# An mLSTM recurrence in chunks: chunk-end maxima found first, each chunk's weights one chunk ahead, loads in two sets

## What is computed

```python
def step(carry, inp):
    C, n, m = carry
    qb, kb, vb, ib, fb = inp
    b = jnp.cumsum(fb, axis=-1)
    d = jnp.where(causal, b[..., :, None] - b[..., None, :] + ib[..., None, :], -jnp.inf)
    inter = b + m[..., None]
    m_t = jnp.maximum(jnp.max(d, axis=-1), inter)
    dexp = jnp.exp(d - m_t[..., None])
    iexp = jnp.exp(inter - m_t)
    s = jnp.einsum('bhtd,bhsd->bhts', qb, kb) * dexp
    num = jnp.einsum('bhts,bhse->bhte', s, vb) + iexp[..., None] * jnp.einsum('bhtd,bhde->bhte', qb, C)
    den = jnp.sum(s, axis=-1) + iexp * jnp.einsum('bhtd,bhd->bht', qb, n)
    h = num / jnp.maximum(jnp.abs(den), jnp.exp(-m_t))[..., None]
    b_last = b[..., -1]
    w_s = b_last[..., None] - b + ib
    m_new = jnp.maximum(b_last + m, jnp.max(w_s, axis=-1))
    wexp = jnp.exp(w_s - m_new[..., None])
    cexp = jnp.exp(b_last + m - m_new)
    C_new = cexp[..., None, None] * C + jnp.einsum('bhs,bhsd,bhse->bhde', wexp, kb, vb)
    n_new = cexp[..., None] * n + jnp.einsum('bhs,bhsd->bhd', wexp, kb)
    return (C_new, n_new, m_new), h
```

## Time and profile before

| | |
|---|---|
| runs of the kernel | 6958.89, 6976.05 and 6981.98 us, median 6976.05 |
| profiled execution, its time | 6989.38 us |
| its span | 6987.6 us |
| mean granted clock of PE | 0.881 of full speed |
| PE busy | 5603.2 us (80%) |
| DVE busy | 2333.7 us (33%) |
| ACT busy | 1178.4 us (17%) |
| DMA moved | 813.87 MB |

### The profile page before, as it was taken

One profiled execution on the slowest core, in us unless ns is written; L12 is line 12 of the kernel. 1 busy time (PEld: TensorE's weight loads), 2 busy tenths in 40 slices (PEclk: granted clock), 3 DMA queues, 4 the chain that ended last, 5 costly groups with the idle time before them and its releaser, 6 DMA issues. The chain is left out here.

```text
span 6987.6 us, 96082 instructions
## 1 busy us (share of the span) xinstructions
PE 5603.2 (80%) x39658; PEld 3068.0 (44%) x39658; DVE 2333.7 (33%) x3925; ACT 1178.4 (17%) x1918; POOL 301.6 (4%) x320
## 2 busy tenths in 40 slices
PE   7998858894986548688859989889558998867778
PEld 4554443332456425233334338888524444322233
DVE  2334310003205643100045365555442120443331
ACT  1222100001110020000023122222201110422111
POOL 0000000001010000000010000000000000211100
PEclk9998869996998757799969999999879999889989
DMA  2110155553133330654332243232231222467721
GB/s 103 36 36 31 60 200 203 220 199 129 48 110 102 111 120 26 244 218 184 146 100 84 80 135 67 53 70 53 73 114 39 57 71 82 145 228 260 254 103 63
DMA packets 559787, 813.87 MB, mean 116 GB/s; under 512 B 176648, under 2 KB 308104, under 8 KB 558920
## 3 DMA queue, kind: packets, MB, share of 16 engines
q1 hardware_dynamic: 491272, 629.25, 27.0%
q0 software_dynamic: 28544, 103.82, 4.2%
q10 hardware_dynamic: 39616, 75.51, 3.0%
HBM read 967.67 MB, written 209.26 MB: 168 GB/s over the span
## 5 line engine op out<-in xcount | busy, mean ns | idle before, releaser
L701 PE MATMUL op_acc<-op_w,op_m 128*128 128x512 f32 x1024 | 451.1, 601 | 63.1 <-DMA op_w<-in_w_out 63.1
L158 PE MATMUL hi_acc<-xT,hi_w 128*128 128x512 f32 x1024 | 445.6, 594 | 8.0 <-DMA hi_w<-in_odd_w_in 8.0
L701 PEld LDWEIGHTS op_acc<-op_w,op_m 128*128 128x128 f32 x1024 | 196.1, 193 | 304.8 <-issue 240.1
L158 PEld LDWEIGHTS hi_acc<-xT,hi_w 128*128 128x128 f32 x1024 | 193.4, 191 | 242.4 <-issue 234.1
L158 PE MATMUL ri_acc<-xT,ri_w 128*128 128x512 f32 (+1 forms) x576 | 253.8, 599 | 10.6 <-DMA ri_w<-in_even_w_in 10.6
L537 PE MATMUL na_acc<-xT,na_w 128*128 128x512 f32 x448 | 219.5, 638 | 40.0 <-DMA na_w<-in_na_w_in 34.0
L158 PE MATMUL di_acc<-xT,di_w 128*128 128x512 f32 x512 | 224.8, 598 | 8.4 <-DMA di_w<-in_even_w_in 8.4
L158 PE MATMUL mi_acc<-xT,mi_w 128*96 128x512 f32 (+1 forms) x512 | 224.3, 598 | 0.0
L3483 PE MATMUL le_gp<-le_g,xT 128*128 128x512 f32 x512 | 220.9, 592 | 0.0
L1183 PE MATMUL moe1e_g_ps<-moe1e_wg,moe1e_xb 128*64 128x512 f32 x768 | 178.9, 620 | 32.9 <-DMA moe1e_wu<-in_exp_w_up 25.7
L1183 PE MATMUL moe0e_g_ps<-moe0e_wg,moe0e_xb 128*64 128x512 f32 x768 | 173.2, 604 | 22.8 <-DMA moe0e_wu<-in_exp_w_up 15.3
(11 more groups left out here) (669 smaller groups left out, 8944.5 us busy)
## 6 DMA issues: line engine op xcount, KB each, us to landing
moe0e_wg<-in_exp_w_gate SPq DMA_DIRECT2D x48, 2048.0 KB
moe0e_wu<-in_exp_w_up SPq DMA_DIRECT2D x48, 2048.0 KB
moe0e_wd<-in_exp_w_down SPq DMA_DIRECT2D x48, 2048.0 KB
moe1e_wg<-in_exp_w_gate SPq DMA_DIRECT2D x48, 2048.0 KB
moe1e_wu<-in_exp_w_up SPq DMA_DIRECT2D x48, 2048.0 KB
moe1e_wd<-in_exp_w_down SPq DMA_DIRECT2D x48, 2048.0 KB
op_m<-scratch_mixedT SPq DMA_DIRECT2D x32, 512.0 KB, 8.8
op_w<-in_w_out SPq DMA_DIRECT2D x32, 512.0 KB, 9.9
```

The costliest lines, as they stand in the source:

```text
L158: mm = pe.matmul(self.acc[i % 2][0:n, h * BANK:(h + 1) * BANK], self.wbuf[i % 3][:, k, 0:n], self.rhs[:, k, h * BANK:(h + 1) * BANK], star ...
L701: mm = pe.matmul(acc[:, n % AHEAD, h * BANK:(h + 1) * BANK], m[:, k, n * P:(n + 1) * P], wb[:, k, h * BANK:(h + 1) * BANK], start=(k == 0) ...
```

## The change

Only `mlstm_scan` changes.

- Before the loop, a, b and the totals of all chunks go into one tile `at` (`[P, 3, NC, U]`). PE turns a once (64 rows of 128 tokens), DVE takes each row's maximum, and a product spreads the 64 maxima over all partitions. Fifteen small operations on DVE then run the recurrence of ML and m over the chunks, and two subtractions with two exps give `cexp` and `wexp` for all chunks.
- The loops are written out over the chunks. While a chunk's numerators are made, the rows of a and M, the maxima, the differences and the scores of the chunk after are made between them; the scores have a PSUM tile `c` of their own, and the weights two tiles.
- a is added to the weights by ACT's exp, as its bias, so the exp is one instruction per unit. ACT also multiplies q times state by iexp, as a copy with a scale; DVE only adds. Both products of a unit lie in one bank.
- q, k, kt, v have two sets. Two chunks are loaded at the start, and the set of chunk t+2 behind the stores of chunk t, once that chunk's states' products are done.

The streams of PE, DVE and ACT (left out: tiles, semaphores, SP's loop and the removed lines):

```diff
+                def number(t, u):
+                    d, h = units[u]
+                    b = u % 2
+                    if u == 0:
+                        pe.wait_ge(W_ready, t + 1)
+                    pe.wait_ge(nums_used, max(t * U + u - 1, 0))
+                    if t:
+                        pe.wait_ge(states_used, (t - 1) * U + u + 1)
+                    pe.matmul(np_[:, b, 0:V], wts[t % 2][:, u, :], vs[t % 2][:, d, h, :], start=True, stop=True)
+                    for j in range(2):
+                        mm = pe.matmul(np_[:, b, V:2 * V], qs[t % 2][:, d, 2 * h + j, :], state[:, u, j, :], start=(j == 0), stop=(j == 1))
+                    mm.then_inc(nums, 1)
...
+                rows_of_a(0)
+                pe.wait_ge(top_found, 1)
+                pe.matmul(cp[:, 4, 0:NC * U], top[:].to_broadcast([NC * U, P]), ident[0:NC * U, 0:NC * U], start=True, stop=True).then_inc(spread, 1)
+                rows_of_M(0)
+                score(0)
+                for t in range(NC):
+                    more = t + 1 < NC
+                    for u in range(2):
+                        number(t, u)
+                    if more:
+                        rows_of_a(t + 1)
+                    for u in range(2, 5):
+                        number(t, u)
+                    if more:
+                        rows_of_M(t + 1)
+                    for u in range(5, U):
+                        number(t, u)
+                    if more:
+                        score(t + 1)
+                    for u in range(U):
+                        update(t, u)
...
+                def weights(t):
+                    act.wait_ge(small_ready, t + 1)
+                    act.activation(small[:, t % 2], small[:, t % 2], ACT.Exp).then_inc(small_exps, 1)
+                    act.wait_ge(D_ready, t + 1)
+                    wt = wts[t % 2]
+                    for u in range(U):
+                        x = act.activation(wt[:, u, :], wt[:, u, :], ACT.Exp, bias=at[:, 0, t, u:u + 1])
+                    x.then_inc(exps, 1)
...
+                for t in range(NC):
+                    for u in range(U):
+                        inter(t, u)
+                        if u == 5 and t + 1 < NC:
+                            weights(t + 1)
+                            act.wait_ge(small_exps, t + 2)
...
+                for t in range(NC):
+                    link(dve.tensor_tensor(ML[:, t, :], ML[:, t, :], mt[:, t, :], ALU.max))
+                    if t + 1 < NC:
+                        link(dve.tensor_tensor(mt[:, t + 1, :], at[:, 2, t, :], ML[:, t, :], ALU.add))
+                link(dve.tensor_tensor(cexp[:], mt[:], ML[:], ALU.subtract))
+                dve.tensor_tensor(wexp[:], at[:, 0], ML[:], ALU.subtract).then_inc(maxima, 1)
...
+                def weigh(t):
+                    dve.wait_ge(exps, t + 1)
                     dve.wait_ge(scores, t + 1)
-                    dve.tensor_tensor(wt[:], wt[:], xp[:], ALU.mult).then_inc(W_ready, 1)
+                    dve.tensor_tensor(wts[t % 2][:], wts[t % 2][:], cp[:], ALU.mult).then_inc(W_ready, 1)
```

More of the change, by code:

```diff
@@ L1537, in mlstm_scan @@
         xp = s.ps("x", [P, U, P])
+        cp = s.ps("c", [P, U, P])
         np_ = s.ps("n", [P, 2, BANK])
-        ip = s.ps("i", [P, 2, BANK])
         sp_ = s.ps("s", [P, 2, BANK])
[L1541 to L1545, removed]
+        names = ("set_up", "mask_loaded", "chain", "tops", "top_found", "spread", "maxima", "chunk_exps", "a_rows", "M_ready", "M_rows",
+                 "D_ready", "small_ready", "small_exps", "exps", "scores", "W_ready", "nums", "inters", "nums_used", "vw_ready",
+                 "states", "states_used", "h_ready", "stored")
+        (set_up, mask_loaded, chain, tops, top_found, spread, maxima, chunk_exps, a_rows, M_ready, M_rows, D_ready, small_ready,
+         small_exps, exps, scores, W_ready, nums, inters, nums_used, vw_ready, states, states_used, h_ready, stored) = (
+             s.sem(n) for n in names)
+        loaded = [s.sem(f"loaded{c}") for c in range(2)]
+        IEXP, EM = range(2)
+        wide = lambda a, n: a.rearrange("p (u a) -> p u a", a=1).to_broadcast([P, a.shape[1], n])
         with s.block() as block:
@@ new lines, in update @@
+                def update(t, u):
+                    d, h = units[u]
+                    b = u % 2
+                    if u == 0:
+                        pe.wait_ge(vw_ready, t + 1)
+                    pe.wait_ge(states_used, max(t * U + u - 1, 0))
+                    for j in range(2):
+                        mm = pe.matmul(sp_[0:QC, b, j * V:(j + 1) * V], kts[t % 2][:, d, (2 * h + j) * QC:(2 * h + j + 1) * QC],
+                                       vw[:, u, :], start=True, stop=True)
+                    mm.then_inc(states, 1)
@@ new lines, in inter @@
+                def inter(t, u):
+                    if u == 0:
+                        act.wait_ge(h_ready, t)
+                    act.wait_ge(nums, t * U + u + 1)
+                    act.activation(num[:, u, :], np_[:, u % 2, V:2 * V], ACT.Copy, scale=small[:, t % 2, IEXP, u:u + 1]).then_inc(inters, 1)
+                act.wait_ge(maxima, 1)
+                act.activation(cexp[:], cexp[:], ACT.Exp).then_inc(chunk_exps, 1)
+                act.activation(wexp[:], wexp[:], ACT.Exp).then_inc(chunk_exps, 1)
@@ L1615, in _ @@
[L1615 to L1624 removed]
+                link = Chain(dve, chain)
@@ new lines, in _ @@
+                for v in vs:
+                    r = dve.memset(v[:], 1.0)
+                    if v is vs[0]:
+                        link(r)
+                r.then_inc(set_up, 1)
+                dve.wait_ge(set_up, 1)
+                link(dve.tensor_copy(at[:, :, :, 0:HEADS], ab[:, :, :, 0, :]))
+                for n in range(NC):
+                    r = dve.tensor_copy(at[:, :, NC - 1 - n, HEADS:U], ab[:, :, n, 1, :])
+                    if n < NC - 1:
+                        link(r)
@@ L1631, in _, with differences @@
+                def differences(t):
                     dve.wait_ge(M_rows, t + 1)
```

194 lines of the change are left out of this document (100 added, 94 removed).

## The result

Four runs of the changed kernel took 6897.8 to 6911.9 us, median **6905.8**. The kernel before, now with four runs, has a median of 6979.01. The ratio is 0.990, with a 95% interval of 0.9877 to 0.9923: 54 to 86 us less. The forecast was 6893.5, the range 6870 to 6926.

The account below looks back on a forecast made before the run. No engine is full; a chain of hand-overs bounds the stage, PE's clock being part of it. Savings of 80.05 us (seven chunks), 1.5 (ahead) and 0.9 (last chunk) make 82.5, from 6976.05 to 6893.5 us; range 6870 to 6926.

Parts of the forecast that it names:

- walk: One loop turn, from one numerator 0 to the next, as nine links in a row: 26.45 us at full clock.
- Chunk: Time per loop turn: 28.0 us, the middle between 26.45 and 29.4; over seven turns 80.05 us less.
- step 4: In the loop on PE: numerator 4, 1.0 us, and the rows of M behind it, 2.05; together 3.05.
- Ahead of the loop: Setup and first chunk: first sums at 12.0 us, numerator 0 at 26.9 instead of 28.4, a gain of 1.5.
- Last chunk: From its numerator 0 to the last state, 18.6 us before: one small operation less and shorter gaps gain 0.9.
- ACT: New forms: 128x193 multiplication 0.43 us, 128x128 exp 0.37; ACT's path 4.9 us against 5.5 on PE, cover 0.6.
- Loads: A set takes 12.3 us and is needed 13.75 us after its request, so it is hidden by 1.4 us.
- A: Rival: waits lower PE's clock; at half clock throughout 7009 us, slower; level at a clock of 0.62; chance 0.04.
- B: Rival: full clock throughout the loop, 26.45 us a chunk, 93 us saved, 6883 us; chance 0.15.
- C: Rival: a load set takes 17 us, scores slip by 3, chunk about 30.5, 65 saved, 6911 us; chance 0.08.
- D: Rival: hand-overs between engines cost 0.25 us more in 16 places, chunk 32, 54 saved, 6922 us; chance 0.10.
- E: Rival: fetching the written-out loops' instructions holds engines up by 11 us a chunk, so no gain; chance 0.03.

Follow-up runs that it names:

- filler: The changed kernel with six unused identity products between numerators 3 and 4, where PE waits 1.66 us: stage 233.3 us against 236.3.
- early_updates: The changed kernel with state updates 0 and 1 moved into PE's wait between numerators 3 and 4, their additions ahead of the differences: stage 214.9 us against 236.3.
- act_more: The changed kernel with `ho` and the weighting of the values moved from DVE to ACT, weighted values in two tiles: stage 212.9 us against 236.3.

## Why the prediction was right, point by point

Numerator 0 came at 2136.49 and 2163.62, so the walk can be laid on the chunk shown above:

| step | forecast, full clock | measured |
|---|---|---|
| 1 numerators 0, 1 | 2.0 | 1.97 |
| 2 rows of a | 2.1 | 1.98 |
| 3 sums, maximum, addition 2 | 3.75 | 3.60 |
| 4 numerator 4, rows of M | 3.05 | 4.71 |
| 5 differences | 1.45 | 1.45 |
| 6 addition 5, numerator 7 | 1.4 | 1.50 |
| 7 scores | 4.1 | 3.87 |
| 8 product, `ho` | 3.1 | 2.80 |
| 9 states | 5.5 | 5.25 |
| sum | 26.45 | 27.13 |

- **Chunk.** Forecast 28.0, the middle between full clock and 0.83; from first to last numerator 0 (2109.25 to 2300.69) it is 27.35. In this turn what the clock costs lies all in step 4, 1.66 us, where the forecast had 1.55 spread over all of PE's terms. The full-clock walk was 1.0 us too long in the other steps. The mechanism is right, waits shortened and the clock up with them; the size of the clock's part is partly luck, for it came from halving the distance between two bounds, and not from anything that says where the clock falls.
- **Ahead of the loop.** First sums at 13.0 us (12.0 forecast), but numerator 0 at 24.7 instead of 26.9: the scores ran at 3.74 us, full clock, where I had 6.2 to 8. A gain of 3.7 us where 1.5 was forecast.
- **Last chunk.** Here the term was wrong in sign: 20.15 us instead of 17.7, and before 18.6. Additions 0 and 1 stand there behind the weighting of the values (1.95), which holds up numerator 2 by 0.87 us, and with nothing between them the numerators come 1.07 us apart, as before; the multiplication on ACT buys nothing in that chunk. The larger part is the clock again: the 24 records of updates took 6.09 us where the last chunk of before took 4.75. Total in the stage 86.8 against 82.5: 84.6 for the chunks against 80.05, and the two small terms off by 2.2 and 2.4 us the opposite ways.
- **ACT.** 0.42 and 0.39 us for the forms taken as 0.43 and 0.37. The exps overlap, 2.46 us for eight instead of 3.0, so from the end of step 5 the denominator was ready in 4.1 us and the scores in 5.4: the cover was 1.3 us instead of 0.6, DVE's wait of 1.26 us for the scores.
- **Loads.** 12.0 us to land, hidden by 3.0 instead of 1.4: no scores of the loop waited for one.
- **Rivals.** A: the clock did fall behind a wait, but only for 3 us or so a chunk, far from the point of 0.62. One reading under A was loose: PE's wait of 2.8 us itself shows a clock of 1.00, and it is the rows of M behind it that show 0.68. The rule of the Trainium skill that spoke for A (TensorE: Matmul & The Clock Gate, A second HAM failure mode: psum-queue depth-cycling) is that a loop which idles briefly and often between groups of matmuls swings between the two levels. The traces agree in part: swings came in loops with waits of 1.7 or 2.3 us, though not behind each, and none at 0.3 to 0.6. B, full clock throughout, was 0.9 us off on the chunk where the forecast was 0.65 off, so it was nearer than its 0.15 says. C did not come, but the argument against it, the same bytes and neighbours, was weak: the same eight pieces took up to 15.5 us in the experiments, and the scores behind them waited. D and E did not come: hand-overs of 0.04 to 0.05 us, no wait for instructions.
- **From stage to program.** The stage lost 86.8 us and the profiled executions differ by 88.9, but the medians differ by 73. The stages ahead of this one, the same code in all kernels, ended between 2069 and 2086 us in these profiles, and what follows took 4558 to 4593. That scatter of 17 us on one side and 35 on the other is enough to hide 14. It also means that the median's distance of 12 us from the forecast, 6905.8 against 6893.5, says little of the walk; the stage does.

## What to carry to other kernels

When no engine is full, write down one turn as a chain of hand-overs, and move every link that does not need the carried state into the waits of the links that do; here taking that order back cost more than half of the gain, and taking back the precomputation that seemed to make it possible almost nothing. A wait of PE can cost twice, once as time and once as clock around it: a third of what the stage lost was PE's own products running faster. Fill it with work that is due anyway; filler won 3.0 us where due work in the same wait, which also left the chain, won 21.4. Price an edit by PE's busy time and its waits apart, over the whole stage, since the drop moves within a turn. A second set of buffers hides only the time between its release and its use, which is to be measured before one trusts it.

## What the runs showed of the hardware that was not expected

- The drop of the clock moves. With the wait of 1.66 us filled, the rows of M went from 0.61 to 1.00, and the updates behind the 2.29 us wait from 1.00 to 0.73. In early_updates the same 2.3 us wait is left, and the updates behind it were slow in one chunk of eight; in act_more the same 1.66 us wait is left, and the rows of M were slow in one of seven. Why is open.
- Two kernels whose loops differ by a link of about 1.1 us had the same 37.59 us per chunk once settled, the difference taken up by where in the chunk PE was slow.
- The loads do not scale with their number: 1.5 us per 384 KB piece for eight in a row, 1.8 for twelve, those of q, k, kt and v 7.2 to 8.0 us from issue to landing in place of 5.0 to 6.0 before. And the same eight pieces took 12.0 us in one set and 15.5 in another.
